# Second block's mixers: where ScalarE and VectorE place splits, exponentials, maxima and head sums between their other steps

## What is computed

```python
def mixer_sublayer(x, n1, w_in_l, qg, kg, rpb_l, og, w_out_l, tables):
    h = rms_norm_2(x, n1)
    proj = h @ w_in_l                      # 1024 -> 2560
    qa, ka, va, qd, kd, vd, qc, kc, vc = jnp.split(proj, cuts, axis=-1)
    qa, ka = rms_norm_2(heads(qa)), rms_norm_2(heads(ka))
    out_a = neighbourhood_attention(qa, ka, va, rpb_l, ...)     # 4 heads
    qd, kd = partial_rotary(rms_norm_2(...)), ...
    out_d = dilated_window_attention(qd, kd, vd, ...)           # 6 heads
    qc, kc = axial_rotary(rms_norm_2(...)), ...
    out_c = gqa_block_attention(qc, kc, vc)                     # 6 heads, 2 key heads
    mix = concat([rms_norm_2(out_a), rms_norm_2(out_d), rms_norm_2(out_c)])
    return x + mix @ w_out_l
```

## Time and profile before

| what | us |
| --- | --- |
| median of 3 runs | 1679.75 |
| lowest and highest run | 1675.15, 1680.56 |
| time of the profiled execution | 1682.92 |
| its span, first to last instruction | 1681.1 |
| PE busy | 1641.7 (98%) |
| DVE busy | 1149.2 (68%) |
| ACT busy | 916.1 (54%) |
| POOL busy | 124.1 (7%) |

### The profile page before, as it was taken

One profiled execution on the slowest core, in us unless ns is written; L12 is line 12 of the kernel. 1 busy time (PEld: TensorE's weight loads), 2 busy tenths in 40 slices (PEclk: granted clock), 3 DMA queues, 4 the chain that ended last, 5 costly groups with the idle time before them and its releaser, 6 DMA issues.

```text
span 1681.1 us, 25493 instructions
## 1 busy us (share of the span) xinstructions
PE 1641.7 (98%) x9631; PEld 1402.2 (83%) x9631; DVE 1149.2 (68%) x1626; ACT 916.1 (54%) x1470; POOL 124.1 (7%) x130
## 2 busy tenths in 40 slices
PE   7999999999999999999999999999999998999999
PEld 6888897888888888997788888877888897778887
DVE  5766656666667666688766666766777777777776
ACT  5444567554445544536754545665655566655554
POOL 0000011000001000150000000140000003110000
PEclk9999999999999999999999999989999999999999
DMA  7555451565555555431155555352555545245552
GB/s 262 200 195 181 150 198 54 213 209 179 197 175 176 196 180 198 175 117 62 53 203 183 192 182 175 109 118 101 196 180 198 177 176 113 100 157 182 177 197 100
DMA packets 42525, 276.76 MB, mean 165 GB/s; under 512 B 7105, under 2 KB 8018, under 8 KB 9554
## 3 DMA queue, kind: packets, MB, share of 16 engines
q1 hardware_dynamic: 40738, 271.00, 46.2%
q0 software_dynamic: 1712, 4.73, 1.6%
HBM read 274.66 MB, written 1.05 MB: 164 GB/s over the span
## 4 chain that ended last, share of the span: by engine, by line
PE 91%; DVE 4%; ACT 3%; POOL 1%; issue 1%; DMA 0%; SPq 0%; DVEq 0%; ACTq 0%; POOLq 0%
PE bank L784 29%; PE bank L802 22%; PE bank L785 14%; PE bank L728 3%; PE bank L687 2%; PE bank L688 2%; PE bank L689 2%; PE bank L935 2%; PE bank L936 1%; PE bank L937 1%; PE bank L1051 1%; PE bank L970 1%; ACT xt_both L1437 1%; PE bank L1052 1%; PE bank L1053 1%; PE bank L850 1%
## 5 line engine op out<-in xcount | busy, mean ns | idle before, releaser
L784 PE MATMUL bank<-xt_both,w_hi 128*128 128x512 f32 x2112 | 747.4, 398 | 5.7 <-DVE xt_both L1924 5.4
L1887 DVE TENSOR_TENSOR w_lo<-raw,w_hi 128x2048 fp32r<-128x2048 f32 (+1 forms) x254 | 580.7, 2286 | 173.0 <-ACT w_hi L1409 172.3
L785 PE MATMUL bank<-xt_both,w_lo 128*128 128x256 f32 x2112 | 590.6, 280 | 0.0
L1409 ACT ACTIVATE w_hi<-raw 128x2048 fp32r<-128x2048 f32 (+1 forms) x254 | 484.8, 1910 | 62.3 <-PE bank L689 41.8
L784 PEld LDWEIGHTS bank<-xt_both,w_hi 128*128 128x128 f32 x2112 | 397.4, 188 | 105.1 <-DVE w_lo L1913 3.7
L785 PEld LDWEIGHTS bank<-xt_both,w_lo 128*128 128x128 f32 x2112 | 399.0, 189 | 2.3
L1632 ACT ACTIVATE KT<-bank 128x256 f32<-128x256 f32 x264 | 86.8, 381 | 339.6 <-PE bank L785 339.6
L802 PE MATMUL bank<-w_hi,h_lo 128*128 128x512 f32 x528 | 208.2, 394 | 0.0
L802 PE MATMUL bank<-w_hi,h_hi 128*128 128x512 f32 x528 | 208.2, 394 | 0.0
L802 PE MATMUL bank<-w_lo,h_hi 128*128 128x512 f32 x528 | 208.2, 394 | 0.0
L802 PEld LDWEIGHTS bank<-w_hi,h_hi 128*128 128x128 f32 x528 | 99.4, 188 | 23.6 <-issue 0.5
(11 more groups left out here) (345 smaller groups left out, 2045.2 us busy)
## 6 DMA issues: line engine op xcount, KB each, us to landing
raw<-in_stream SPq DMA_DIRECT2D x255, 1024.0 KB, 4.9
work<-in_rpb POOLq DMA_DIRECT2D x32, 64.0 KB, 3.6
X<-in_x SPq DMA_DIRECT2D x2, 512.0 KB, 4.9
prob<-in_cmp_w POOLq DMA_DIRECT2D x1, 1024.0 KB, 7.1
O<-in_cmp_w POOLq DMA_DIRECT2D x1, 1024.0 KB, 12.1
out<-X SPq DMA_DIRECT2D x4, 256.0 KB, 2.0
cst<-in_consts SPq DMA_DIRECT2D x1, 712.0 KB, 10.5
O<-in_final_gain POOLq DMA_DIRECT2D x1, 512.0 KB, 5.9
```

The lines of the kernel that those rows point to most:

```text
L784: pe.matmul(both, w_hi[:, sl, cols], xt_both[:, :, k, :], start=(k == 0), stop=False)
L785: ins = pe.matmul(dst[:, 0:S], w_lo[:, sl, cols], xt_hi[:, k, :], start=False, stop=(k == KD - 1))
L1409: act.activation(to, src, ACT.Copy).then_inc(hi_done, 1)
L1887: dve.tensor_tensor(to, src, hi.bitcast(F32), ALU.subtract).then_inc(lo_done, 1)
```

## The change

In both layers of the second block's mixer:

- ScalarE splits unit u0+6 between `evac(3)` and `evac(4)` instead of behind `tiles(1)`. It does `exponentials(0)` ahead of the split of u0+7, and `turned(0)`, `exponentials(1)` and `turned(1)` ahead of the split of u0+8.
- VectorE splits unit u0+6 right behind u0+5, ahead of `keys_high` and `maxima(0)`. It does `head_sums(1)` right behind `maxima(0)` instead of behind `maxima(1)`, and `prepare(1, 0)` ahead of `maxima(2)` instead of behind it.
- TensorE does 6 of the 24 matmuls of `half(7, 1)` ahead of `transposes(2)`, 9 ahead of `transposes(4)` and the last 9 behind it (before: none, 12, and 12).

In layer 0 alone, VectorE waits for `rstd_done` to reach 8, which is GpSimd's root and product, before its split of u0+3.

In the first block's first mixer, ScalarE's eight squares (L1832) and its two copies of transposed query tiles (L1690) are interleaved in another way: 2 squares, a copy, 1 square, a copy, 5 squares, instead of 4 squares, both copies, 4 squares.

```diff
--- before.py
+++ after.py
@@ -1086,11 +1086,12 @@
                 values(0)
                 half(7, 0)
                 turn_p(3)
+                half(7, 1, 0, 2)
                 transposes(2)
                 transposes(3)
-                half(7, 1, 0, 4)
+                half(7, 1, 2, 5)
                 transposes(4)
-                half(7, 1, 4, KD)
+                half(7, 1, 5, KD)
 
                 scores(3)
                 turn_p(4)
@@ -1554,19 +1555,19 @@
                 evac(2)
                 split(u0 + 5)
                 evac(3)
+                split(u0 + 6)
                 evac(4)
                 tiles(0)
                 tiles(1)
-                split(u0 + 6)
                 head_squares(1)
+                exponentials(0)
                 split(u0 + 7)
-                exponentials(0)
                 evac(5)
-                split(u0 + 8)
 
                 turned(0)
                 exponentials(1)
                 turned(1)
+                split(u0 + 8)
                 evac(6)
                 split(u0 + 9)
 
@@ -1825,9 +1826,9 @@
             for t in range(NT):
                 act.activation(O[:, t, 0:512], bank[2 + t][:, :], ACT.Copy).then_inc(mla_kv, 1)
 
-            def out_squares(t):
-
-                for h in range(GLA_H):
+            def out_squares(t, h0=0, h1=GLA_H):
+
+                for h in range(h0, h1):
                     src = bank[GLA_O_BANKS[h % 2]][:, (2 * t + h // 2) * P:(2 * t + h // 2 + 1) * P]
                     act.activation(KT[:, 2816:2944], src, ACT.Square, accum_out=ss[:, 16 + t * 4 + h:17 + t * 4 + h]).then_inc(g_sq, 1)
                     if 4 * t + h < 7:
@@ -1836,8 +1837,11 @@
             split(U["mix0"])
             split(U["mix0"] + 1)
             act.wait_ge(g_o, 1)
-            out_squares(0)
-            feature_major("mla", 1)
+            out_squares(0, 0, 2)
+            feature_major("mla", 1, 3)
+            out_squares(0, 2, 3)
+            feature_major("mla", 3)
+            out_squares(0, 3)
             out_squares(1)
 
             def gla_out_hi():
@@ -2032,24 +2036,26 @@
                     if t == 1:
                         dve.sem_inc(ft_ready_d, 1)
 
+                if l == 0:
+                    dve.wait_ge(rstd_done, 8)
                 split(u0 + 3)
                 head_sums(0)
                 split(u0 + 4)
                 prepare(0, 0)
                 prepare(0, 1)
                 split(u0 + 5)
+                split(u0 + 6)
                 keys_high()
                 maxima(0)
-                split(u0 + 6)
+                head_sums(1)
 
                 scale(0)
                 maxima(1)
-                head_sums(1)
                 split(u0 + 7)
 
                 scale(1)
+                prepare(1, 0)
                 maxima(2)
-                prepare(1, 0)
                 prepare(1, 1)
 
                 scale(2)
```

## The result

The changed kernel takes 1662.45 us (median of 4 runs, 1661.81 to 1663.44), the kernel before, run beside it, 1680.15 (1675.15 to 1682.04). The ratio is 0.9903, with a 95% interval of 0.9890 to 0.9917: faster by 0.8 to 1.1%. The prediction said 1664, between 1659 and 1671. The profiled execution took 1663.44 us, its span is 1661.6 us against 1681.1 before, and 19.5 us of span have to be found.

The account below looks back on a forecast made before the run. TensorE, busy 98% of the span, was taken as the bound. Waits of 11.1 us and clock of 7.0 gave 1664.8 from 1682.92; counting 5 of clock, 1679.75 - 16 = 1664 us, range 1659 to 1671.

Parts of the forecast that it names:

- The sum: Whole kernel: 11.1 us of waits plus 7.0 of clock off 1682.92, giving 1664.8; for the median, 16 off 1679.75.
- the fourth outcome: Rival, chance 0.04: GpSimd's root blocks VectorE for 4.2 us, scale(0) comes late in both layers, 1674 us.
- Part 1: Layer 0 start: VectorE's split of u0+3 waits for the root; wait for transposes(0) falls 2.49 to 0.5 us.
- Part 2: Both layers: moving the split of u0+6 is free on ScalarE, at most a new 0.4 us wait in layer 0.
- Part 3: ScalarE's exponentials ahead of splits, both layers: the 2.80 us wait at scores(1) of layer 1 goes whole.
- Part 4: Earlier sums of kind 1, root behind them: waits of 3.73 and 2.86 us for prepare(1, 1) go in layers 0 and 1.
- The tie I forecast: At transposes(2), VectorE's chain ends nearly when TensorE asks, 0 to 0.3 us to spare in layer 0.
- Part 5: First block's squares and tile copies: counted 0, between -0.2 and +0.3 us; TensorE's 0.88 us wait shrinks by up to 0.2.
- The clock gave its share back: Answers a rival, chance 0.22: clock gives nothing or a tie fails; gain 9 to 12 us, 1669.
- The wait for the root works: Answers a rival, chance 0.06: layer 0's root takes 2.68 us whatever VectorE does; 1668 us.
- The root of 24 did not hold VectorE: Answers the rival of a root blocking VectorE 4.2 us at scale(0) or a split; chance 0.04, 1674.
- The bias fetch: Rival, slower, chance 0.04: GpSimd's 16 DMAs start 11 us earlier and block a stream load; 1684 us.

Follow-up runs that it names:

- the three with one part alone: Kernel before plus one change each: VectorE's wait for the root, 1674.56 us; split of u0+6 moved, 1674.47; earlier sums, prepare(1, 0) and TensorE's matmuls, 1674.00.
- the one with u0+6 back: Changed kernel with the split of u0+6 back in its old places on ScalarE and VectorE: 1667.48 us.
- the one with late sums: Changed kernel with head_sums(1) behind maxima(1) again, prepare(1, 0) still ahead of maxima(2): 1674.22 us.
- the wait alone: Kernel before with VectorE's wait for the root ahead of layer 0's split of u0+3 as its one change: 1674.56 us.

## Why the prediction was right, point by point

**The sum.** I expected 11.1 us of waits and 7.0 of clock off the profiled execution, 1664.8 us. It was 1663.44. TensorE's waits in the two stretches fell from 13.2 to 2.1 us, by the 11.1 expected, and the other 7.5 of the 18.6 us there I put down to the clock, which fell three times in them before and never after. The sum was 1.4 us short: these 0.5, and the 1.4 of the fall of the clock near 1127 us in the kernel before, which I had not priced, less the 0.5 lost ahead of the mixer. That fall comes 2.3 to 2.7 us behind the start of the twelve short matmuls of L1020 (1124.53). It stands there in layer 0 of the kernel before and of the three with one part alone, in layer 1 of the changed kernel without the wait, of the one with u0+6 back and of the one with late sums, and in neither layer of the changed kernel. Why is open. For the median I counted 5 of the 7 us of clock, 16 us in all; it fell by 17.3, from 1679.75 to 1662.45. The 0.93 for a gain of over 0.3% holds only a quarter of the fourth outcome's 0.04, not most of it.

**Part 1** was right in each row: the root 0.70 us, the wait 0.52 us (0.5), and the clock stayed up. The 2.8 us of clock that I priced there are real for TensorE's work (12.31 - 1.30 = 11.0 us before from `transposes(0)` to `scores(1)`, 9.97 - 1.30 - 0.31 = 8.4 after), but worth less than that on their own, since next to waits for other engines slow work is partly free.

**Part 2** is where a step failed. I called the move free and gave it nothing but a wait of 0.4 us (it came, 0.31). It was free where it went, and yet undoing it costs 5.3 us. In layer 0 it is 3.2 us, since the split then stands between the sums and `scale(0)`: a wait of 2.04 us at `turn_p(0)` and a fall of the clock. In layer 1 it is 2.1 us, 1.02 of them at `scores(1)` and 0.94 at `turn_p(0)`. I had these us in the sum, under parts 3 and 4, because I worked out the chains of ScalarE and VectorE with the split already away. The sum was right and its division wrong.

**Part 3** was predicted as 2.80 us in layer 1 and a tie in layer 0. Undone alone it costs 1.0 us and nothing, because moving u0+6 has already taken 1.8 us off the same wait.

**Part 4** was right in size and in mechanism: 3.73 and 2.86 us went, and the undone sums bring 3.74 and 3.73 back. The tie I forecast came as a tie: VectorE's last step ended 0.23 us before TensorE asked (I had 0 to 0.3), the root took 4.16 us (4.2), and taking 0.7 us of matmuls away made TensorE wait 0.46.

**Part 5** I put between -0.2 and +0.3 us. The waits came that way, 0.13 shorter and 0.41 longer. I did not see that falls of the clock would come with the longer one, 1.56 us, in five executions of seven. Four of them cost about half a us.

**The rivals.** The clock gave its share back. The wait for the root works. The root of 24 did not hold VectorE: the split at 1081.88 began inside it and took 2.28 us,

```profile
1079.42 0.62 DVE L1996 TENSOR_SCALAR prob<-prob,rsum 128x256 f32<-128x256 f32 x2
...
1081.88 2.28 DVE L1891 TENSOR_TENSOR w_lo<-raw,w_hi 128x2048 fp32r<-128x2048 f32 x1
```

and `scale(0)` beside its start took 0.62 us. Beside GpSimd's 16 DMA issues the two pairs of scalings of `scale(1)` took 0.69 and 0.76 us instead of 0.62, which my chain did not have; the 0.23 us to spare are what was left with them in it. The bias fetch landed in 6.2 us instead of 3.6, the stream's loads in 4.9 as before, and no wait for one appeared.

## What to carry to other kernels

When several engines share a schedule with no slack, price a move by the chain it leaves, not only by the gap it goes into, and undo each part in the result before you say which one paid: here undoing the move I called free costs 5.3 us and undoing the one I credited 1.1, and of the wait that both shorten whichever is made first takes the larger share. Moves lean on one another, too, since an early root pays fully only if no split is queued between it and the scaling. And read a stretch between two marks of the critical engine beside the total: it told 1 us from nothing where medians of four runs could not. It does so only where the clock stays up in it: for the parts made alone it mixes waits with falls of the clock.

## What the runs showed of the hardware

**A split holds a root that starts behind it; the reverse did not show.** A root that began 0.17 us behind a split of 2.29 us took 6.14 instead of 4.16 us for 24 numbers, in six kernels with the one before, and 2.67 instead of 0.70 for 2. A scaling of 0.62 us that began with a root took its usual time, and so did every split that began while a root was running, and the root stayed at 4.16. The Trainium skill, SBUF — State Buffer, "Who interferes with whom", calls the shared pair of ports an exclusive lock. For a split that comes first the rows agree. For a root that comes first they do not, and the measurement decides here, but only for what it covers: these splits began 1.65 us or more into the root, and none began earlier.

**Falls of the clock go with waits of TensorE, but not by their length alone.** Of the kernels profiled, six have no wait over 1.3 us in either mixer, and in all six the clock was full through both mixers. It fell behind 2.04, 2.50, 2.79, 3.25 and 3.74 us. But it did not behind the 3.26 us of layer 1 with u0+6 moved alone, nor behind the 2.86 us of layer 1 in the kernel before and with the wait alone, and behind the 1.56 us of the first block it fell in some executions of like kernels and not in others. What a wait costs with its fall is read from the runs: without the wait for the root 1.98 us of wait at `transposes(0)` cost 3.5, with late sums 7.5 us cost 12.0.
